# Dilated attention on one core: value products with the values stationary, and the merge of the three groups moved into the steps of the last one

## The reference, cut to what matters

```python
for g, (win, dil) in enumerate(ATTN_GROUPS):
    o, lse = dilated_prompt(q[:, :, g], k[:, :, g], v[:, :, g], dil, win // dil)
    outs.append(o); lses.append(lse)
wts = jax.nn.softmax(jnp.stack(lses, axis=0), axis=0)
o = jnp.sum(wts[..., None] * jnp.stack(outs, axis=0), axis=0)
return jnp.einsum('bte,ed->btd', o.reshape(B, T, 8 * 64), w_o)
```

## Time and profile before

| | |
|---|---|
| time, median of 3 runs | 2184.47 us (2184.27 to 2188.75) |
| the profiled execution | 2183.8 us, span 2182.0 us |
| TensorE (PE) busy | 2139.0 us, 98% |
| VectorE (DVE) / ScalarE (ACT) / GpSimd (POOL) busy | 1538.6 / 981.6 / 508.6 us |
| chain that ended last | PE 94%, DVE 3%, ACT 1%, DMA 1%, issue 1% |

### The profile page before, as it was taken

How to read it: one execution, slowest core, us unless ns; L and a number is a source line. 1 busy time by engine, 2 the same in 40 slices (tenths; PEclk the granted TensorE clock), 3 DMA queues, 4 the chain that set the end, 5 groups by cost and what they waited for, 6 DMA issues and landing times.

```text
span 2182.0 us, 42756 instructions
## 1 busy us (share of the span) xinstructions
PE 2139.0 (98%) x15928; PEld 2007.2 (92%) x15939; DVE 1538.6 (71%) x2327; ACT 981.6 (45%) x1854; POOL 508.6 (23%) x722
## 2 busy tenths in 40 slices
PE   7999999999999999999999899899999999999998
PEld 7999999999999977777777788699999999999998
DVE  4888888888656677465564567777888888885554
ACT  4655555555435532122121445456555555554332
POOL 1002223222100155455454100010122233221000
PEclk8999999999999999999999999899999999999999
DMA  6236787788985522523534457641467877899664
GB/s 191 88 98 171 188 210 193 192 213 229 320 253 183 169 96 78 179 83 108 160 105 148 147 180 224 183 138 59 145 164 203 208 195 202 211 257 315 204 200 145
DMA packets 242191, 383.74 MB, mean 176 GB/s; under 512 B 22008, under 2 KB 118936, under 8 KB 240167
## 3 DMA queue, kind: packets, MB, share of 16 engines
q1 hardware_dynamic: 201862, 273.15, 38.3%
q0 software_dynamic: 34912, 104.20, 21.3%
q10 hardware_dynamic: 5288, 4.68, 0.6%
HBM read 304.10 MB, written 174.43 MB: 219 GB/s over the span
## 4 chain that ended last, share of the span: by engine, by line
PE 94%; DVE 3%; ACT 1%; DMA 1%; issue 1%; SPq 0%; ACTq 0%; DVEq 0%
PE ps L1253 40%; PE ps L1356 20%; PE ps L2159 6%; PE ps L2161 6%; PE ps L2160 6%; PE ps L2401 2%; PE ps L2792 2%; PE ps L2374 2%; PE ps L2385 1%; PE ps L423 1%; PE ps L2341 1%; PE ps L864 1%; PE ps L488 1%; PE ps L2153 1%; PE ps L2154 1%
## 5 line engine op out<-in xcount | busy, mean ns | idle before, releaser
L1253 PE MATMUL ps<-hT,w 128*128 128x258 f32 x2752 | 458.4, 283 | 0.5 <-DVE ua L1486 0.5
L1253 PEld LDWEIGHTS ps<-hT,w 128*128 128x128 f32 x2752 | 384.9, 189 | 1.2 <-issue 0.6
L1253 PE MATMUL ps<-lT,w 128*128 128x258 f32 x1376 | 276.3, 282 | 0.0
L1253 PE MATMUL ps<-hB,w 128*128 128x258 f32 x1344 | 229.3, 282 | 0.0
L2159 PE MATMUL ps<-wq,xh 128*128 128x512 f32 x576 | 227.6, 395 | 0.7 <-DVE wq L1946 0.7
L2161 PE MATMUL ps<-wq,xl 128*128 128x512 f32 x576 | 227.4, 395 | 0.0
L2160 PE MATMUL ps<-wq,xh 128*128 128x512 f32 x576 | 226.9, 394 | 0.0
L1253 PEld LDWEIGHTS ps<-lT,w 128*128 128x128 f32 x1376 | 213.3, 189 | 0.0
L1356 PE MATMUL ps<-gdh,wda 128*128 128x258 f32 x1184 | 198.7, 283 | 0.0
L1356 PE MATMUL ps<-gdh,wdb 128*128 128x258 f32 x1152 | 193.5, 284 | 0.3
L1253 PEld LDWEIGHTS ps<-hB,w 128*128 128x128 f32 x1344 | 191.0, 189 | 0.0
(11 more groups left out here) (345 smaller groups left out, 4824.5 us busy)
## 6 DMA issues: line engine op xcount, KB each, us to landing
stage<-in_w_up SPq DMA_DIRECT2D x176, 256.0 KB, 3.7
wsum<-in_w_down POOLq DMA_DIRECT2D x132, 256.0 KB, 5.4
gs<-cb SPq DMA_DIRECT2D x44, 516.0 KB, 6.8
stage<-wsum SPq DMA_DIRECT2D x88, 256.0 KB, 2.9
tsum<-gs POOLq DMA_DIRECT2D x66, 258.0 KB, 7.7
tsum<-gneg POOLq DMA_DIRECT2D x66, 258.0 KB, 8.3
stage<-in_w_down SPq DMA_DIRECT2D x58, 256.0 KB, 3.2
stage<-in_w_kv SPq DMA_DIRECT2D x24, 512.0 KB, 4.2
```

Source lines behind the costliest of these rows:

```text
L1253: mm = pe.matmul(ps[:, bank + c, 0:HB], w, m[:, c * HB:(c + 1) * HB], start=(first and i == 0), stop=(i == len(parts) - 1), skip_group_che ...
```

## The change

- **Order.** `STEPS` now begins with group 1 (8 steps), then group 2 (8), and group 0 comes last: its tiles are neighbouring tokens, so the token tiles are complete one after the other. The sample work moves with it: half steps 10 to 31.
- **Value products.** 64 value columns are stationary, the 128 columns of the turned probabilities stream; even heads write partitions 0 to 63, odd heads 64 to 127 of the same columns of PSUM. The outputs are born turned (channel on the partition, token along the row).
- **Outputs stay on chip.** VectorE copies them into `outT` (groups 1 and 2, scattered to their tokens with a stride of 4 or 16 elements) or `osb` (group 0). Only maxima and sums of groups 1 and 2 go to DRAM (`ost`, 64 B a row) and come back in one DMA issued by GpSimd.
- **Merge in the steps.** From half step 36 on, for token tile t in half steps 36 + 2t and 37 + 2t: VectorE makes the weights, GpSimd widens them to 64 columns a head (four copies), TensorE turns them into PSUM (6 transposes a half step, in banks 6 and 7), VectorE multiplies the outputs in place, GpSimd adds the three groups, ScalarE rounds, GpSimd makes the low part. The transposes of merged outputs (L2805, L2806) are gone.
- **Other moves.** ScalarE copies the turned q tiles of the last group. GpSimd makes w_o's low parts. Two of the four early w_o chunks run in TensorE's iterations 48 and 49, two at the head of `pe_merge`; the sample turns are in iteration 51. The sample values are loaded in steps 2 to 9 and 15 of SP's list, three w_o pieces at 15 and the fourth at 20.

```diff
-        STEPS = [(0, n, 0, n > 0) for n in range(8)] + [(1, n, r, n > 0) for r in range(4) for n in range(2)] + \
-            [(2, s, 0, False) for s in range(8)]
+        STEPS = [(1, n, r, n > 0) for r in range(4) for n in range(2)] + [(2, s, 0, False) for s in range(8)] + \
+            [(0, n, 0, n > 0) for n in range(8)]
+        LOCAL = 2 * 8
...
-        H_NEW, H_SM = 28, 33
+        H_NEW, H_SM = 10, 17
...
+        V_AT = {2: (0, 1, 2), 3: (3, 4, 5), 4: (6, 7, 8), 5: (9, 10, 11), 6: (12, 13, 14), 7: (15, 16), 9: (17, 18),
+                15: (19, 20, 21, 22, 23)}
...
-        VALUES_AT = {40: (0, 0), 41: (0, 1), 42: (0, 2), 44: (1, 0), 45: (1, 1), 46: (1, 2)}
-        DIAGONAL_AT = 43
+        VALUES_AT = {24: (0, 0), 25: (0, 1), 26: (0, 2), 28: (1, 0), 29: (1, 1), 30: (1, 2)}
+        DIAGONAL_AT = {27: 0, 31: 1}
...
+        def out_columns(i):
+            g, n, r, _ = STEPS[i // 2]
+            pairs = slice(2 * (i % 2), 2 * (i % 2) + 2)
+            src = ps[:, 6, 0:HW].rearrange("p (c q) -> p c q", c=2)
+            if g == 1:
+                return outT[:, 0, pairs, 0:T].rearrange("p c (m r) -> p c r m", r=4)[:, :, r, n * P:(n + 1) * P], src
+            if g == 2:
+                return (outT[:, 1, pairs, 0:T].rearrange("p c (u r) -> p c r u", r=16)[:, :, 2 * n:2 * n + 2, :],
+                        src.rearrange("p c (r u) -> p c r u", r=2))
+            return osb[:, n % 3, pairs, :], src
...
-                        v = kv_tile(tile)[:, QW + h * HD:QW + (h + 1) * HD]
-                        mm = pe.matmul(ps[:, 6, j * HD:(j + 1) * HD], probT[:, i % 2, n * P:(n + 1) * P], v,
-                                       start=(w == 0), stop=(w == len(tiles) - 1))
+                        for odd in range(2):
+                            h = 4 * (i % 2) + 2 * pair + odd
+                            n = (2 * pair + odd) * len(tiles) + w
+                            mm = pe.matmul(ps[64 * odd:64 * odd + 64, 6, pair * P:(pair + 1) * P],
+                                           kv_tile(tile)[:, QW + h * HD:QW + (h + 1) * HD], probT[:, i % 2, n * P:(n + 1) * P],
+                                           start=(w == 0), stop=(w == len(tiles) - 1), tile_position=(0, 64 * odd),
+                                           skip_group_check=True)
...
+            def weights(t, second):
+                pe.wait_ge(mg_b, 4 * t + 1 + 2 * second)
...
+                spread(t, 0, (2, 3) if second else (0, 1), 6, HW)
+                wait(pe, mg_m, MULTS * t + 2 * second)
+                pe.wait_ge(at_tc, 2 * min(LOCAL + 3 + t, NSTEP - 1) + (2 if second or t >= 5 else 1))
+                pe.wait_ge(mg_b, 4 * t + 2 + 2 * second)
+                spread(t, 2 if second else 1, range(4), 7, 0)
...
+            def weighted(t, second):
+                v.wait_ge(at_oc, 2 * (LOCAL + t + 1))
+                v.wait_ge(mg_t, MULTS * t + (3 if second else 1))
+                own = osb[:, t % 3, 2 * second:2 * second + 2, :]
+                nc.vector.tensor_tensor(own, own, ps[:, 6, HW:QW].rearrange("p (c q) -> p c q", c=2),
+                                        ALU.mult).then_inc(mg_m, 1)
+                v.wait_ge(mg_t, MULTS * t + (4 if second else 2))
+                far = outT[:, second, :, tok]
+                nc.vector.tensor_tensor(far, far, ps[:, 7, :].rearrange("p (c q) -> p c q", c=4), ALU.mult).then_inc(mg_m, 1)
...
+                if i >= 2 * LOCAL + 6 and i % 2 == 0:
+                    act_high_merged(act, (i - 2 * LOCAL - 6) // 2)
...
+            def widen(t):
+                q.wait_ge(mg_v, MG * (t + 1))
+                for second in range(2):
+                    if t:
+                        q.wait_ge(mg_t, MULTS * (t - 1) + 2 + 2 * second)
+                    for first, n in ((4 * second, 4), (HEADS * (1 + second), HEADS)):
+                        nc.gpsimd.tensor_copy(wb[:, first * HD:(first + n) * HD].rearrange("p (h e) -> p h e", h=n),
+                                              ow[:, t % 2, 3, first:first + n].unsqueeze(2).to_broadcast([P, n, HD])).then_inc(mg_b, 1)
...
+            for t in range(7):
+                widen(t + 1)
+                own = osb[:, t % 3, :, :]
+                for second in range(2):
+                    q.wait_ge(mg_m, MULTS * t + 3 + second)
+                    wait(q, mg_s, SUMS_M * t + second)
+                    nc.gpsimd.tensor_tensor(own, own, outT[:, second, :, t * P:(t + 1) * P], ALU.add).then_inc(mg_s, 1)
+                if t == 3:
+                    low_wo(3)
+                low_merged(q, nc.gpsimd, t)
```

More of the change, by code:

```diff
@@ new lines, in build, with stats_of, store_stats @@
+        VALUES_AT = {24: (0, 0), 25: (0, 1), 26: (0, 2), 28: (1, 0), 29: (1, 1), 30: (1, 2)}
+        DIAGONAL_AT = {27: 0, 31: 1}
+        def stats_of(s):
+            return st[:, s, :] if s < LOCAL else sg[:, s - LOCAL, 0, :]
+        def store_stats(e, s):
+            e.wait_ge(at_e, 2 * s + 2)
+            for part, dst in tile_rows(ost[:, STEPS[s][0] - 1, :], s):
+                e.dma_start(dst, st[part, s, :]).then_inc(st_out, 16)
+        ST_OUT = 16 * sum(dmas(s) for s in range(LOCAL))
@@ L2315, in scores_out, with load_wo @@
+        def load_wo(e, k):
+            e.dma_start(stage[:, k % 3, :], a["w_o"][0, k * P:(k + 1) * P, :]).then_inc(piece_in[k % 3], 16)
         def scores_out(i):
@@ L2403, in outputs @@
-                mm.then_inc(at_o, 1)
+                t, second = merge_at(i + 2)
+                if t is not None and 2 * t + second:
+                    pe.wait_ge(mg_m, MULTS * t + 1 if second else MULTS * t - 1)
+                tiles = [s - 1, s] if wide(i) else [s]
+                for pair in range(2):
+                    for w, tile in enumerate(tiles):
+                        for odd in range(2):
[5 more added lines that the diff above has]
+                                           skip_group_check=True)
@@ L2471, in outs @@
                 v.wait_ge(at_o, i + 1)
-                nc.vector.tensor_copy(osb[:, i // 2 % 3, HW * (i % 2):HW * (i % 2) + HW], ps[:, 6, 0:HW]).then_inc(at_oc, 1)
-            for i in range(NH + 2):
+                t, second = merge_at(i + 2)
+                if t is not None:
+                    v.wait_ge(mg_t, MULTS * t + (3 if second else 1))
+                if i == 2 * LOCAL:
+                    v.wait_ge(sm_new, 9)
+                tile = i // 2 - LOCAL
+                if tile >= 3:
+                    v.wait_ge(mg_l, tile - 2)
@@ L2475, in dve_attention @@
+            for i in range(NH + 4):
                 if i < NH:
                     maxima(i)
-                if i // 2 + 1 < NSTEP:
+                if i // 2 + 1 < NSTEP and (i % 2 or i < 2 * LOCAL):
                     turned(i // 2 + 1, i % 2)
@@ L2831, in pe_merge @@
                     pe.wait_ge(wo_x, WO_FREE[i])
-                columns(d, range(first, NC), b)
+                wo_columns(pe, d, range(first, NC), b)
         @block.sync
```

437 lines of the change are left out of this document (201 added, 236 removed).

## The result

The changed kernel takes 2159.64 us (median of 4 runs, 2157.86 to 2162.49) against 2184.37 us of the kernel before on the same chip (4 runs): ratio 0.9883, 95% interval 0.9865 to 0.9901. The forecast was 2155.3, so it is 4.3 us too low, within its range of 2146 to 2175. The spans of the two profiled executions, 2182.0 and 2159.3 us, differ by 22.7.

The account below looks back on a forecast made before the run. TensorE was taken to bound the kernel (94% of the chain). Value products -19.0, late loads +3.5, merge in the steps +8.3 and the end -22 gave -29.2; 2183.8 - 29.2 + 0.7 = 2155.3 us, range 2146 to 2175.

Parts of the forecast that it names:

- Value products, -19.0: Attention steps: turned value products priced like score products, 1.73 to 1.09 us wide, 0.84 to 0.65 narrow; 19.0 us off.
- Rival (b): Value products: the two heads' products run one after the other, the 19.0 us saving is gone, 2174 us; chance 0.10.
- The fixed price per group: Score and value products: a fixed 0.21 us per group, taken as tiling mode cost; without it 10 us more saved.
- Late loads, +3.5: Start of the last group: q and kv loads queued behind others on SP, and late statistics, cost 3.5 us, ends 0 and 10.
- The merge in the steps, +8.3: From half step 36: TensorE's weight transposes, 0.69 us a set, twelve of sixteen sets inside the steps, add 8.3 us.
- After the last product, -22: Between last value product and main w_o product: 43.5 us shrink to 21, early w_o columns at half clock; 22 us off.
- GpSimd, 8.7 us a block: Last group: GpSimd's widening, sums and low part, 3072 columns at 2.85 ns, take 8.7 us of a 9.5 us token block.
- Rival (a): Last group: GpSimd mildly sets the pace through rounding and exponentials, 5.6 us per half step, +10 us, 2165; chance 0.20.
- rival (c): Last group: GpSimd is the bound at 14.1 us a block, eight blocks add 37 us, 2192 us, slower; chance 0.08.
- The break-even: Last group: GpSimd's block time from which it decides whether the kernel gets slower, 9.5 + 29/8 = 13.1 us.
- Strided copies, 0 with an end of 5: VectorE's output copies with stride 4 or 16, 32 of 48: counted as nothing, at most some 5 us.
- its case: Whole kernel: the forecast's main case, 2155.3 us with its own range 2149 to 2161; chance 0.52.

## Why the prediction was right, and where its steps were off

**Value products, -19.0: right in kind, 1.7 too large.** The products alone gained more than was said: 8 cost 1.02 (forecast 1.09), 4 cost 0.59 (0.65), which makes 22 x 0.71 + 26 x 0.25 = 22.1. But the transposes of probabilities ahead of them cost 0.10 more in each of the 48 half steps, a term that the forecast put at nothing. That leaves 22.1 - 4.8 = 17.3. Rival (b), no side by side, would have cost 10.8 us and not 19.0: its "0.21 each as now" was too high for the serial form too, which takes 1.51 for 8.

The fixed price per group isn't settled. 8 products at 1.02 and 4 at 0.59 differ by 0.43, which would leave 0.16 per group, near the 0.21 of the scores. The serial form, in the same tiles, has 1.51 and 0.60, and by the same working no fixed part at all. The Trainium skill (TensorEngine Tiling, Key Properties) says that a change of tiling mode drains the array. The 0.10 stands where full-width transposes are followed by products in column tiles and is absent where full-width products follow, which is in keeping with that; but the two kernels differ in more than the tiles there, so that it is a drain isn't shown.

**Late loads, +3.5: about right, in another place.** In the profiled run they cost 5.3 us in half steps 29 and 30, in the six experiments with the same loads 1.6 to 4.1. The text named the q and kv loads queued behind the values, and those were in time; it was the values themselves that TensorE waited for. Moving them one step removed it.

**The start, not in the forecast: +1.7.** From half step 0 to half step 2 it is 11.9 us against 10.2, since TensorE waited 6.3 us for its first q tile instead of 4.2. The load was issued 0.7 later, at 1211.69 instead of 1210.99, and TensorE went on 3.9 after that instead of 2.6. The tile now holds every fourth token; whether this makes its transfer longer was not tried.

**The merge in the steps, +8.3: too small.** A set of six transposes costs 0.71 (forecast 0.69), and 13 sets lie ahead of the last value product's end, not 12: 9.2. The text also left out that two early w_o columns (1.89 each) now run in iterations 48 and 49, before the last product: 3.8. They cover little there. Before, TensorE had only these waits in the same iterations, 1.5 us:

```profile
1399.66 0.66 PE L2385 MATMUL ps<-ident,prob 128*128 128x128 f32 x4 [0.91 <-ACT prob L2560]
...
1401.76 1.08 PE L2401 MATMUL ps<-kvt,probT 128*128 128x64 f32 x8 [0.61 <-DVE osb L2472]
```

These columns, 2.3 us net, are the largest term that the forecast left out.

**The steps together.** -17.3 + 5.3 + 1.7 + 9.2 + 3.8 - 1.5 = 1.2 against the measured 1.0.

**After the last product, -22: right by 2, partly by luck.** Measured -24.1. Up to the end of the last set of transposes it took 14.2 us where the forecast's pieces give 12.3: the sample turns take 8.1 us at half clock instead of 6.5, and three sets of transposes lie here instead of two. From there the w_o product with its two early columns took 43.1 us where the forecast's pieces give 46.5. The forecast counted 3.8 for the last multiplies, sums, rounding and low part and 5 more for the columns, one behind the other; they run beside each other, and half clock costs the w_o product only 1.6 (43.09 for 264, against 41.5 at 0.157 each). The errors offset each other in part. The run with the turns earlier shows that 5.3 us of this stretch were a matter of order.

**GpSimd, 8.7 us a block: too high.** It took 5.8. The copies cost 0.40 us for 256 columns and 0.61 for 512, half of a sum or less (1.27). Rival (a) did not occur: with GpSimd's work raised by 2 us a block, nothing happened in the steps before half step 46. With 6 us more per block the kernel was slower than before, as rival (c) said, but on the path that rival (a) describes, through the rounding and the exponentials: GpSimd works 12.1 of the 13.6 us. The break-even was put at 13.1 us a block; the run with 13.6 us, 6.6 us over the kernel before, gives an estimate of 13.6 - 6.6 / 8 = 12.8. The change works at 9.6.

**Strided copies, 0 with an end of 5: right.** 5.9 us more on VectorE, at most 0.6 on TensorE's path.

**The sum.** -29.2 against -23.1: 8.2 short in the steps, 2.1 too careful behind them. The 8.2 are the value products (1.7), the late loads (1.8), the start (1.7), the weights (0.9) and the columns (2.3), less 0.2. The rest, that the forecast sign and its case held with a chance of 0.52, rests on the same rows: TensorE was the bound before and is the bound after.

## What to carry to other kernels

When work is moved from a stage of its own into the steps of the bounding engine, count everything that moves with it, fillers too: an instruction that covered a wait in its old place costs its full time in the new one. Small operations under which the granted clock falls belong directly behind dense work and in a gap that is there anyway; here one line moved was worth 5.3 us. When the shape of a product changes, read the cost of a whole half step and not of the product alone: the transposes ahead of it became 0.10 dearer each time. And before a late load is blamed for delaying what is queued behind it, look whether its own reader is the one that waits; then compare stretches of the traces and not only medians, because such waits vary by 2 us from one execution to the next: doubling GpSimd's copies cost 3.1 us in the trace and nothing in the median.

## What the runs showed of the hardware that was not expected

- Two heads side by side in TensorE's columns pay only in the longer group: 8 products 1.51 to 1.02 us, 4 products 0.60 to 0.59.
- GpSimd's copy of a weight broadcast over 64 columns costs 1.2 ns a column at 512 columns and 1.6 at 256, its sum of two tiles 2.5 (1.27 us for 512), with VectorE busy beside it.
- VectorE's copy out of PSUM costs 0.60 us with a destination stride of 4 or 16 elements, 0.41 without.
- The granted clock did not stay up through the 32 small sample turns, though they followed each other without a gap. Behind dense work 9 to 13 of the 16 pairs ran at 0.31 us and the rest at 0.52 (five profiles). Behind the wait of 2.3 us all ran at 0.52 in the changed kernel, at a granted clock of 0.50 (1.2 GHz); with the values loaded earlier the first six ran at 0.31.
- The transposes ahead of the value products take 0.10 us longer when the products are in column tiles: 0.43 to 0.53 for four, 0.87 to 0.97 for eight.
